# An encoder trunk of retention and attention on eight cores: q projections of later blocks among the softmax's matmuls, transposes further back, first loads reordered

## The reference, cut to what matters

```
u = rms_norm(h, g0); q, k, v, g = split(u @ w_in)          # layer 0: retention, 4 heads, qk 256, v 512
q, k = rope(q), rope(k) / 16
y = forward scan + backward scan of (q . k) decay v         # chunkwise
h = h + (silu(g) * group_norm(y)) @ w_out
h = h + relu(rms_norm(h, g1) @ w1)**2 @ w2                  # d_ff 4096
q, k, v = split(rms_norm(h, g2) @ w_in)                     # layer 1: 8 q heads, 2 kv heads of 128
q = rope(rms_norm(q, q_gain)) * 128**-0.5;  k = rope(rms_norm(k, k_gain))
h = h + (softmax(q k^T) v) @ w_out
h = h + relu(rms_norm(h, g3) @ w1)**2 @ w2
return rms_norm(h, g4)
```

## Time and profile before

| | us |
|---|---|
| median of the runs shown (3) | 4478.2 |
| the runs shown | 4478.2, 4281.2, 4831.0 |
| the profiled execution | 4292.3 |
| its slowest core's span (core 7) | 4290.6 |
| spans of the eight cores | 4265.2 to 4290.6 |
| granted clock, eight cores | 0.977 to 0.982 |

### The profile page before, as it was taken

The page is one execution under the profiler, slowest core; times in us unless marked ns, Lnnn a source line. Parts: engine busy times, 40 slices in busy tenths (PEclk is TensorE's granted clock), DMA queues, the critical chain, the costliest instruction groups (busy, mean ns, idle before and its releaser), DMA issues.

```text
span 4290.6 us, 64381 instructions; the slowest of 8 cores (4265.2 to 4290.6 us)
## 1 busy us (share of the span) xinstructions
PE 3909.5 (91%) x22464; PEld 1936.3 (45%) x22464; DVE 1742.5 (41%) x2478; ACT 1738.2 (41%) x2915; POOL 997.8 (23%) x846
## 2 busy tenths in 40 slices
PE   2798898999997989999988998899999879999999
PEld 1344444444443655444434444444444445554444
DVE  2556653222255233322375556532223632342224
ACT  3344543311154877111245444432113467751113
POOL 2345341111125000111223444301111430001111
PEclk8999999999999999999999999999999999999999
DMA  8332224422223000222352322243222220002211
GB/s 171 72 59 61 44 55 128 96 40 40 40 52 63 3 1 1 55 40 40 64 163 45 62 52 60 64 146 59 40 40 42 43 52 1 1 14 46 40 20 79
DMA packets 199019, 235.56 MB, mean 55 GB/s; under 512 B 10672, under 2 KB 148144, under 8 KB 198704
## 3 DMA queue, kind: packets, MB, share of 16 engines
q0 software_dynamic: 96032, 111.16, 17.3%
q1 hardware_dynamic: 102672, 120.28, 9.2%
HBM read 304.81 MB, written 37.75 MB: 80 GB/s over the span
## 4 chain that ended last, share of the span: by engine, by line
PE 70%; DVE 10%; issue 7%; ACT 6%; DMA 4%; POOL 2%; SPq 1%; DVEq 0%; ACTq 0%; POOLq 0%
PE psall L311 68%; DVE sb_M L331 5%; ACT sb_M L327 4%; DMA sb_M<-x 3%; PE psall L317 2%; POOL sb_M L331 2%; DVE sb_M L343 2%; DVE sb_st L797 1%; DVE sb_st L966 1%; ACT sb_st L327 1%; ACT sb_M L348 1%; DMA sb_M<-qkg 1%; DVE sb_U L343 1%; SPq L359 1%; ACT sb_U L327 1%
## 5 line engine op out<-in xcount | busy, mean ns | idle before, releaser
L327 ACT ACTIVATE sb_M<-psall 128x512 f32<-128x512 f32 (+1 forms) x1216 | 933.6, 781 | 1342.5 <-PE psall L311 1222.1
L331 POOL TENSOR_TENSOR sb_M<-sb_M 128x512 bf16<-128x512 f32 (+3 forms) x696 | 834.0, 1211 | 1959.8 <-ACT sb_M L327 1367.2
L311 PE MATMUL psall<-sb_uT,sb_ring 128*128 128x512 bf16 x5120 | 1121.6, 381 | 57.1 <-DVE sb_M L331 54.5
L311 PE MATMUL psall<-sb_ring,sb_M 128*128 128x512 bf16 x5120 | 1129.6, 381 | 9.4 <-DMA sb_M<-yg_scr 9.3
L311 PE MATMUL psall<-sb_ring,sb_uT 128*128 128x512 bf16 x3328 | 824.2, 381 | 0.4 <-DVE sb_M L331 0.2
L311 PEld LDWEIGHTS psall<-sb_uT,sb_ring 128*128 128x128 bf16 x5120 | 500.1, 98 | 660.4 <-issue 68.2
L311 PEld LDWEIGHTS psall<-sb_ring,sb_M 128*128 128x128 bf16 x5120 | 498.9, 98 | 605.1 <-issue 22.4
L331 DVE TENSOR_TENSOR sb_M<-sb_M,psall 128x1024 f32<-128x1024 f32 (+1 forms) x352 | 395.4, 1124 | 811.9 <-PE psall L311 725.9
L311 PE MATMUL psall<-sb_M 128*128 128x129 bf16 (+2 forms) x5504 | 647.3, 258 | 73.1 <-DVE sb_st L1033 46.1
L311 PEld LDWEIGHTS psall<-sb_M 128*128 128x128 bf16 x5504 | 411.9, 98 | 344.8 <-issue 144.6
L331 DVE TENSOR_TENSOR sb_M<-psall,sb_M 128x512 f32<-128x512 f32 (+3 forms) x576 | 383.6, 715 | 276.7 <-ACT sb_M L327 131.3
(11 more groups left out here) (41 smaller groups left out, 1397.9 us busy)
## 6 DMA issues: line engine op xcount, KB each, us to landing
sb_ring<-mlp_w POOLq DMA_DIRECT2D x64, 1024.0 KB, 13.1
sb_M<-x SPq DMA_DIRECT2D x64, 512.0 KB, 9.2
sb_ring<-ret_w_in POOLq DMA_DIRECT2D x16, 1024.0 KB, 12.1
yg_scr<-sb_M SPq DMA_DIRECT2D x64, 256.0 KB, 2.3
sb_M<-yg_scr SPq DMA_DIRECT2D x16, 1024.0 KB, 8.0
y<-sb_M SPq DMA_DIRECT2D x32, 512.0 KB, 2.9
sb_ring<-ret_w_in POOLq DMA_DIRECT2D x16, 512.0 KB, 10.9
sb_M<-cos_r SPq DMA_DIRECT2D x32, 256.0 KB, 4.5
```

Of the source, the lines that this page charges most:

```text
L311: self.S.op("pe", lambda e: e.matmul(out.ap, lhsT.ap, rhs.ap, start=start, stop=stop, **kw), reads=_k(lhsT, rhs), writes=_k(out))
L327: return e.activation(out.ap, in_.ap, func, scale=_a(scale), **kw)
L331: self.S.op(eng, lambda e: e.tensor_tensor(out.ap, in0.ap, in1.ap, op=op), reads=_k(in0, in1), writes=_k(out))
```

## The change

1. **Start.** Only weight slot 0 is issued at once; slots 1, 2 and 3 are issued on POOL when x chunk 9, 12 and 15 have landed, 4 and 5 also behind chunk 15. The x buffers are five, placed where they don't lie on the rope's temporaries, so for the first sequence the x work is written ahead of the ropes no more. `tab_load(0)` and `(1)` stand behind the fourth chunk, the constant table behind the sixteenth.
2. **Attention tables.** They are made in the first sequence's first MLP, from its first w2 stage on, in eight steps 12 us apart on the scheduler's clock: two loads, four POOL products of 128 x 256, a write of 512 KB.
3. **Gated product.** `trans` of `ret_fwd` is written 6.6 us behind the gate, not 5.0.
4. **Attention.** `inproj` and `attn_core` become `attention`. K and V are projected for all blocks first, two blocks at a time (`kv_pair`: 16 matmuls, 128 x 512 operations, one table buffer). q is projected by `q_pieces`, 16 single matmuls per block, the block's products by halves. Blocks 0 to 3 are done among the first two pairs, blocks 4 to 15 become filler, in a queue with the output projection: q 4 to 11, output 0, q 12 to 15, then outputs 1 and 2. A step gets one filler matmul, the last of a head five, 12 per head in all 32 heads. q's `uT` copy is on VectorE in the core. `evict`'s transposes come 3.0 us later, not 2.2. The table buffers lie on the constant table, which is loaded again after the core. The weight order is K/V, q, q.

```diff
-                    for i in range(3):
+                    for i in (2, 0, 1):
                         loads.append(("cols", wa_in, [(0, i * 512, 512)]))
...
-        XS0 = M(R0 + 16 * KB, [4, D], F32)
+        XS0 = M(8 * KB, [5, D], F32)
-        XP0 = Pool(B, xsl + [XS0.v(i) for i in range(4)])
+        XP0 = Pool(B, [XS0.v(i) for i in range(5)])
...
                     if h == 0:
-                        B.ensure(*[("xs", s, c) for c in range(16)])
                         if s > 0:
+                            B.ensure(*[("xs", s, c) for c in range(16)])
...
-                    B.at(5.0, lambda i=i, b=b, bt=bt: trans(i, b, bt))
+                    B.at(6.6, lambda i=i, b=b, bt=bt: trans(i, b, bt))
...
+        def kv_pair(c, w):
+            need_u(c, c + 1)
+            KR = KRs[c // 2 % 2]
+            B.dma("sp", TK.v(), at_d[c * 128:(c + 2) * 128, 256:512]..., key="tk", ...)
+            b = B.pair()
+            for j in range(2):
+                for k in range(8):
+                    B.mm(PS(b + j), uT.v(k, ((c + j) * 128, (c + j + 1) * 128)), w(k, 0, 512), k == 0, k == 7)
...
+            B.at(2.4, stat)
+            B.at(5.0, trans)
+        def q_pieces(c, ws, ev):
...
+                            if hf == 0:
+                                need_u(c)
+                                if c >= 2:
+                                    B.ensure(("q", c - 2))
+                                B.dma("sp", TQ.v(sl), at_d[c * 128:(c + 1) * 128, 0:256]..., key=("tq", sl), ...)
+                            st["b"] = B.bank()
...
+                B.act(qr.v(hs), pq, AF.Square)
+                for i, dst in ((0, a), (1, Bq)):
+                    B.tt("dve", dst.v(hs), pq, ..., ALU.mult)
+                B.give(b)
...
+                B.at(4.0, stat)
                 B.at(8.5, trans)
...
+            for c in range(0, 16, 2):
+                kv_pair(c, wkv)
+                if c < 4:
+                    for cc in (c, c + 1):
+                        for p in q_pieces(cc, wq, "act"):
+                            p()
...
+            for c in range(4, 12):
+                fill.extend(qp[c - 4])
...
                     if h == 7:
-                        outproj(qb)
-                elif fill:
-                    fill.pop(0)()
-                    if len(fill) > (N - n) or (fill and i == 3):
-                        fill.pop(0)()
+                        fill.extend(outproj(qb))
+                        if qb == 0:
+                            for c in range(12, 16):
+                                fill.extend(qp[c - 4])
+                            fill.append(wq_done)
+                    run(5)
+                else:
+                    run(1)
...
-        for _ in range(NRING):
-            w_issue()
+        w_issue()
         g0 = load_gain(0)
         for c in range(16):
             load_c(0, c, g0, "act" if c % 2 else "dve")
+            if c == 3:
+                tab_load(0)
+                tab_load(1)
+            if c in (9, 12, 15):
+                w_issue([("xsd", c)])
+        B.dma("sp", CT.v(), ctab_d[:, 0:NCT - 128], key="ctab")
+        for _ in range(NRING - 4):
+            w_issue([("xsd", 15)])
```

More of the change, by code:

```diff
@@ L489, in build, with w_issue @@
         wst = {"issued": 0, "taken": 0, "released": 0}
-        def w_issue():
+        def w_issue(after=()):
             i = wst["issued"]
@@ L503, in w_issue @@
                     B.dma("pool", V(vw.ap, [("ringh", s, j)] if len(arg) == 2 else [("ringh", s, 0), ("ringh", s, 1)]),
-                          src[:, :, s0:s0 + n], key=("ring", s, j))
+                          src[:, :, s0:s0 + n], key=("ring", s, j), reads=after)
             else:
@@ L691, in ret_qk @@
             w_release(1)
+            if h == 0:
+                B.ensure(*[("xs", s, c) for c in range(16)])
         def ktr(h, b):
@@ new lines, in build, with bc @@
+        Aq = [M(R0 + 24832 + i * 4096, [8, 128], F32) for i in range(2)]
+        Bq = M(R0 + 33024, [8, 128], F32)
+        QR = [M(R0 + 37120 + i * 2048, [8, 128], BF16) for i in range(2)]
+        Ak = M(R0 + 41216, [2, 2, 128], F32)
+        Bk = M(R0 + 43264, [2, 2, 128], F32)
+        KRs = [M(R0 + 45312 + i * 1024, [2, 2, 128], BF16) for i in range(2)]
+        TK = Buf(Cz, "C", 0, [2, 2, 128], F32, 16)
+        TQ = Buf(Cz, "C", 2048, [2, 2, 128], F32, 16)
+        def bc(v, ap):
+            return V(ap, v.keys)
@@ L991, in rope @@
-                B.at(3.0, fin)
-                B.at(8.5, trans)
-            for c in range(16):
-                need_u(c)
-                bq, bk = B.pair(), B.bank()
-                for k in range(8):
-                    for n in range(3):
-                        bb = bq + n if n < 2 else bk
-                        B.mm(PS(bb), uT.v(k, (c * 128, (c + 1) * 128)), ws[n](k, 0, 512), k == 0, k == 7)
-                rope(c, bq, bk)
-            w_release(3)
-            for c in range(16):
-                B.ensure(("qk", c))
@@ L1005, in inproj, with trans @@
-            for c in range(16):
-                B.done.discard(("qk", c))
-        def attn_core(g):
+                B.tt("pool", kr, Ak.v(), bc(ss, ss.ap.rearrange("p (a b) -> p a b", a=2).unsqueeze(3)
+                                            .to_broadcast([128, 2, 2, 128])), ALU.mult)
+            def trans():
+                bb = B.bank()
+                for j in range(2):
+                    for h in range(2):
+                        B.tr(V(PSb(bb)[:, (h * 2 + j) * 128:(h * 2 + j + 1) * 128], [("ps", bb)]), KR.v(j, h), ident)
+                B.cp("act", kTa.v(None, (c * 128, (c + 2) * 128)),
+                     V(PSb(bb)[:, 0:512].rearrange("p (h t) -> p h t", h=2), [("ps", bb)]))
+                B.give(bb)
+                B.done.add(("k", c))
+                B.done.add(("k", c + 1))
@@ new lines, in attention @@
+        def attention(g):
+            for i in range(16):
+                B.done.discard(("k", i))
+                B.done.discard(("q", i))
+            B.memset("dve", va.v(None, None, (128, 130)), 1.0)
+            wkv = w_next()
+            wq = [w_next() for _ in range(2)]
+            for c in range(0, 16, 2):
[4 more added lines that the diff above has]
+                            p()
+            w_release(1)
@@ L1010, in attn_core @@
             wo = [w_next() for _ in range(2)]
-            fresh_u()
             sc = 128.0 ** -0.5
-            fill = []
-            for b in range(6):
-                B.take(b)
+            fill = collections.deque()
             def S_(n):
@@ L1020, in S_ @@
                 bk = 2 * (n % 2)
+                if h == 0:
+                    while any(("q", qb * 4 + j) not in B.done for j in range(4)):
+                        if fill:
+                            fill.popleft()()
+                        else:
+                            B.ensure(*[("q", qb * 4 + j) for j in range(4)])
+                B.ensure(("k", 2 * i), ("k", 2 * i + 1))
                 for j in range(2):
@@ L1045, in trans @@
                     B.done.add(("oT", qb, h))
-                B.at(2.2, trans)
+                B.at(3.0, trans)
             def outproj(qb):
+                out = []
                 for i in range(4):
@@ L1058, in one @@
                                         B.ensure(*[("oT", c // 4, hh) for hh in range(8)])
+                                        for i in range(4):
+                                            B.done.discard(("uT", c + i))
                                     st["b"] = B.bank()
@@ L1067, in one, with wq_done @@
                                         norm_c(X.v(c), c, g, "dve", "dve")
-                            fill.append(one)
+                            out.append(one)
+                return out
             N = 256
+            total = 12 * 16 + 3 * 64
+            qp = [q_pieces(c, wq, "dve") for c in range(4, 16)]
+            def wq_done():
+                w_release(2)
+            for c in range(4, 12):
+                fill.extend(qp[c - 4])
+            for b in range(6):
+                B.take(b)
             S_(0)
@@ L1073, in attn_core, with run @@
             po = 4
+            acc = 0.0
+            done = 0
+            def run(k):
+                nonlocal done
+                for _ in range(k):
+                    if fill:
+                        fill.popleft()()
+                        done += 1
             for n in range(N):
@@ L1149, in build @@
             g2 = load_gain(2)
-            mlp(lambda c: norm_c(X.v(c), c, g2))
-            inproj()
+            mlp(lambda c: norm_c(X.v(c), c, g2), early=at_tables if s == 0 else None)
             g3 = load_gain(3)
-            rest = attn_core(g3)
+            rest = attention(g3)
             g4 = load_gain(4)
```

161 lines of the change are left out of this document (88 added, 73 removed).

## The result

| | before | after |
|---|---|---|
| median of the runs shown (4 each) | 4383.2 us | 4292.2 us |
| the profiled execution | 4292.3 us | 4106.3 us |
| its slowest core's span | 4290.6 us (core 7) | 4104.7 us (core 4) |
| granted clock, eight cores | 0.977 to 0.982 | 0.988 to 0.992 |

In several executions of either kernel one die ran at a lower clock, and they lift both medians; the comparison leaves them out. The ratio of after to before is 0.959, 95% interval 0.954 to 0.964: faster. The forecast was 4069 us, range 3990 to 4180. The profiled execution lies in the range; the median of the runs, 4292.2, lies outside. In the forecast's terms 186 us were won where 223 were promised, and 4069/4292.3 = 0.948 is outside the interval of the ratio too.

What follows compares the result with a forecast made beforehand. TensorE, busy 91% of the span, was taken as the bound, so only its idle time and stages paced by other engines could be won. 62 + 63 + 98 = 223 off 4292.3 gave 4069 us, range 3990 to 4180.

Steps and rivals of the forecast that it cites:

- The start, 62: Kernel start: TensorE's 54.46 us gap goes, K's first transposes come at 86 instead of 148; 62 us won, bounds 70 and 45.
- four products of 0.61, one of 1.2 on POOL and a queue's pause: Start: rope work taken to stand between the 115 projection matmuls, ending at 82, and K's transposes at 86.
- The tables in the MLP, 0: First MLP: making the attention tables there costs 0, covered by result buffers and banks; 24 us without that cover.
- The gated product, 63: Retention heads: later transposes win three quarters of 86 us of TensorE's waits for POOL, edges included; bounds 86 and -10.
- The first rival: Heads: waits return at matmuls needing a cast or bank, and the start wins 45; 153 us won, 4139; chance 0.17.
- The attention layer, 98: Projection and core: 465.0 becomes 58 before first scores plus 358 core, 49 saved per sequence, 98 for two; best 172, worst none.
- The allowance of 0.2 for ScalarE: Attention core, each head: ScalarE's squares hold exponentials up, 0.2 us within a head of 11.2.
- q transposes of blocks 0 and 1 are forced early by the reuse of their buffers: Attention, before first scores: transposes forced while POOL still has rope products in its row; 8 us of the 58.
- (2): Attention core bound by evictions: 1.5 us more a head, the layer wins nothing; 125 us won, 4167; chance 0.14.
- (3): Core clock kept low by new bank waits: change lost at 34% of core work at 1.2 GHz, 4362 at 45%; chance 0.03.
- (4): Start: x and weights hold the stage, so 62 us becomes 30, 4101; chance 0.08.
- Ports: Attention core: VectorE and POOL lock shared SBUF ports; 4 us expected, inside the 0.3 per head, 102 in all at worst.

Runs made afterwards that it cites:

- Experiments 2 and 4: The first: before with the gated product's transposes at 6.6 instead of 5.0, 4240.5 us. The second: after with the transposed product's copy on VectorE, not ScalarE, 4093.1 us.
- experiment 3: After with the gated product's transposes back at 5.0 in the first three heads, 6.6 only in the last: 4135.4 us.
- experiment 7: After with the norm root's logarithm and exponential queued 2.6 us later on ScalarE where VectorE makes the sum of squares: 4075.8 us.
- experiment 8: Two kernels, one edit each on after: second table buffer for K, 4109.1 us; four early q projections spread over four K/V pairs, 4094.2 us.
- experiment 10: After with all five edits of the kernel with five edits, and the gated product's transposes at 8.0 us instead of 6.6: 4048.3 us.
- the kernel with five edits: After with q's weight release joined, product copy on VectorE, later norm root, q projections spread, second K table buffer: 4034.0 us.

## Why the prediction was right or wrong

**The terms it was given in.** The failing step is "I forecast in its terms". The profiled execution of before was near the lowest of its runs, and a median is taken over executions that the rows don't describe. The line says 4069 with 4180 as its upper end; the median came out at 4292.2. The forecast should have been put as a ratio to before. Counted in its own terms, 4106.3 lies inside the range, and what is off is in the terms below.

**The start, 62: measured 56.5.** The mechanism held: no gap, no weight held it, x's last transposes at 57.00 where 57 was forecast. The 115 matmuls took 26.1 us for 24.8. The mis-sized term is "four products of 0.61, one of 1.2 on POOL and a queue's pause", 4.0 us. What stands behind the 115 matmuls is another row: TensorE's own 32 matmuls of V's projection, which the sum left out. They run from 83.94 to 90.85, 6.9 us, in before as in after (139.07, 7.07 us). Of VectorE's and GpSimd's work 0.82 us comes out ahead of K's transposes on core 4, and none on four of the eight cores. The late table pair that the prediction feared did come, 14.2 us from issue to use, and VectorE stood 1.16 and 1.94 us for its two tables; TensorE had its 32 matmuls meanwhile and lost next to nothing. In the median of the cores the start won 52.9, since core 7 of before was the latest of its eight.

**The tables in the MLP, 0: right.** 450.05 and 450.10 us from MLP to projection.

**The gated product, 63: measured 60.7,** but not where it was looked for. "I take three quarters" of the waits in the heads: there 16.5 + 18.0 = 34.5 us were won, about half of the 76 us of GpSimd's waits. The first rival had the reason: 24.0 us of waits for a ScalarE copy stand in the first sequence's heads. That copy is queued behind the next gate's three activations and, in the row shown, the next head's decay factors too. Experiments 2 and 4 show the copy; 4 wins 13 by moving it. The prediction priced such waits by their length; the clock behind them, 0.50 for the 12 matmuls behind the stop of 3.33, it did not price. The other 26 us came behind the heads, where the prediction had only "the heads' edges"; experiment 3 shows that the last head's own move makes them. The two errors, some 28 and 26 us, cancelled; that the term is nearly right is luck. Below 15 us of waits for GpSimd per sequence, as forecast: 3.2 and 4.6.

**The attention layer, 98: measured 38.4 + 46.9 = 85.3, less 14.0 behind it, 71.3.** "The layer's 465.0 becomes 58 + 358 = 416". The prediction cut at the first scores: there it is 62.9 + 363.7, each some 5 us over. From the second scores on, 1233.10 to 1591.09, the core is 358.0 like the sum, but by parts that are not. Its heads with q as filler take 10.7 us and those with output matmuls about 12. The allowance of 0.2 for ScalarE counted its squares, which hold up little; what held exponentials up was the norm's root, two activations of 0.6 us together with a wait of some 2 us ahead of them (experiment 7: 20.6 and 17.0 us of the layer). The eviction waits fell to 2.7 us in all, as forecast. The first part, to the end of the last stop, took 68.6 where 58 stood: "q transposes of blocks 0 and 1 are forced early by the reuse of their buffers", 8 us, was the right cause at less than its price. TensorE is idle there for 17.2 us, where 13 were allowed, and its own work took 51.4 us, not 45, at a granted clock of 0.91 that the sum took as full. Spread out, the stretch is 6 us shorter in the median (experiment 8). K's table, given 3 us, is worth nothing that a second buffer could win. And the 14.0 us behind the core were in no term: one entry too many in a queue of 384 places. It could be counted in the diff: 12 x 16 + 3 x 64 pieces, and `wq_done` appended as one more.

**The handover, -2.7:** in no term, and within what cores differ by (1.7 won in the median). The shortfall is thus 5.5 + 2.3 + 26.7 + 2.7 = 37 us, the 223 less the 186.

**The rivals.** (1) came half true in the heads and fully in experiment 10. (2), eviction as the bound, fell. (3) fell: the clock in the core was 0.98 to 1.00. Behind the core groups did cycle through one bank, with 0.84 us of idle each, and the clock was 1.00 there. The oscillation of which the Trainium skill tells ("TensorE: Matmul & The Clock Gate", § A second HAM failure mode: psum-queue depth-cycling) did not show in it. The 0.96 of the earlier trace rows is six heads of some 12 us, granted 0.86 each, and in all six the clock fell behind a stop of 1.58 us at the head's end. In after, with five filler matmuls there, no such stop is left. (4) fell with the gap.

**Ports.** The 4 us for VectorE and GpSimd holding each other up can't be told from these runs: GpSimd is busy 34.7 of 122 us while q is the filler, and 0.00 in the last window, where the output blocks' norm steps run. They hardly meet.

## What to carry to other kernels

On an engine that works strictly in order, price not only what is added but what waits inside it: two activations of one column, written ahead of the work they do not depend on, cost 17 to 21 us a layer, and moving them 2.6 us back won 31 with no instruction less. A stop of TensorE can cost more than it lasts: look at the granted clock of the matmuls behind it. Before the work of one engine is added to a path, list what the other engine has in the same stretch: here 32 matmuls hid a late table. Read a stage on all cores before comparing it. When filler is dealt out in fixed places, count the entries, the bookkeeping ones too: one left over held a bank through the next stage. A wait that is moved by writing work further back ends at the next buffer that this work holds, so move it until the other name grows, and stop there.

## What the runs showed of the hardware

The same instruction list does not take the same time on eight cores without data between them: in one execution of the kernel with five edits the MLP took 449.8 us on every core, while retention's first output projection took 118.7 us on core 0 and 128.9 on core 3. On core 0 TensorE's longest stop in it was 1.04 us and the granted clock 1.00; on core 3 one stop was 4.66 us, for a norm's result from VectorE, and the clock 0.97. What made that result late on core 3 is not shown. The time is that of the slowest core, so gains of a few microseconds in one stage can vanish behind such a spread.

Behind stops of TensorE of 3.33, 4.98 and 5.03 us the granted clock was 0.50 for the next matmuls. In the core of before it fell behind six stops of 1.58 us (0.86 over each of these heads), while in after's core heads with a stop of 1.68 us were granted 1.00, and so was the stretch with repeated stops of 0.84 us. The length of one stop alone does not tell whether the clock falls.
